# Second block of a two-block transformer layer: the q_b projection tiles go last, preparation of the delta chunks moves beside them, ScalarE takes the key scalings, and TensorE's chunk work is reordered

## What is computed

```python
proj = h @ w_in
(qkv_a, z_a, b_a, a_a, q_b, ckv, z_b, iq, ik, iw) = split(proj)
qkv = silu(causal_conv(qkv_a, conv_w)); q, k, v = split(qkv)
q = l2norm(q) * DK ** -0.5; k = l2norm(k); beta = sigmoid(b_a)
g  = -exp(a_log) * softplus(a_a + dt_bias); gc = cumsum(g)          # in each chunk
decay = exp(where(causal, gc[:, None] - gc[None, :], -inf))
lmat  = where(strict, (k * beta) @ k.T * decay, 0)                  # then (I + lmat)^-1
attn  = (q @ k.T) * decay
qg = q * exp(gc);  kg = k * exp(gc[-1] - gc);  vb = v * beta;  kb_g = k * beta * exp(gc)
```

## Time and profile before

| | |
|---|---|
| median of 3 runs | 2002.6 us (2000.28 to 2003.87) |
| the profiled execution | 1995.06 us, span 1992.9 us, mean granted TensorE clock 0.963 |
| busy in the span | PE 1866.0 us (94%), DVE 1514.0 (76%), ACT 1118.4 (56%), POOL 194.1 (10%) |
| the twelve last split tiles | to about 1762 us of the span |
| biases, g sums, four chunks | about 1762 to 1814 us |
| doubling and the attention of the second mixer | about 1814 to 1930 us |

### The profile page before, as it was taken

One profiled execution on the slowest core, in us unless ns is written; L12 is line 12 of the kernel. 1 busy time (PEld: TensorE's weight loads), 2 busy tenths in 40 slices (PEclk: granted clock), 3 DMA queues, 4 the chain that ended last, 5 costly groups with the idle time before them and its releaser, 6 DMA issues. The chain is left out here.

```text
span 1992.9 us, 24544 instructions
## 1 busy us (share of the span) xinstructions
PE 1866.0 (94%) x8417; PEld 1398.4 (70%) x8418; DVE 1514.0 (76%) x1725; ACT 1118.4 (56%) x1162; POOL 194.1 (10%) x199
## 2 busy tenths in 40 slices
PE   6978978999999999999999999999998999977998
PEld 3346456787777777777787777778774467866983
DVE  4146666999999899899999988998896377866532
ACT  4233315777777777777777767777754344322510
POOL 0031210000000000000000000000143001003410
PEclk9988978999999999999999999999998889988999
DMA  7100836999999999999999999999977212201001
GB/s 211 65 21 11 341 137 226 373 360 369 376 352 368 384 359 373 375 356 374 378 365 377 377 352 371 376 353 383 361 265 239 81 43 70 79 0 64 1 22 42
DMA packets 102007, 499.72 MB, mean 251 GB/s; under 512 B 18611, under 2 KB 35232, under 8 KB 51684
## 3 DMA queue, kind: packets, MB, share of 16 engines
q1 hardware_dynamic: 94898, 473.37, 62.0%
q0 software_dynamic: 7056, 25.69, 3.6%
HBM read 478.57 MB, written 20.46 MB: 250 GB/s over the span
## 5 line engine op out<-in xcount | busy, mean ns | idle before, releaser
L1627 DVE TENSOR_TENSOR part<-ring,part 128x2048 fp32r<-128x2048 f32 x380 | 858.1, 2289 | 108.6 <-ACT part L1348 107.6
L1348 ACT ACTIVATE part<-ring 128x2048 fp32r<-128x2048 f32 x380 | 729.1, 1921 | 331.8 <-DMA ring<-in_w_gate_up 192.2
L1477 PE MATMUL bank<-part,xT_hi 128*128 128x512 f32 x2048 | 535.0, 403 | 20.1 <-DVE xT_lo L1658 15.2
L1477 PEld LDWEIGHTS bank<-part,xT_hi 128*128 128x128 f32 x2048 | 380.9, 190 | 116.0 <-issue 30.6
L1488 PE MATMUL bank<-part,actT_hi 128*128 128x512 f32 x1024 | 280.4, 395 | 0.3 <-ACT rest L1371 0.3
L1477 PE MATMUL bank<-part,xT_lo 128*128 128x512 f32 x1024 | 280.2, 395 | 0.0
L1477 PEld LDWEIGHTS bank<-part,xT_lo 128*128 128x128 f32 x1024 | 193.2, 189 | 45.7
L1488 PEld LDWEIGHTS bank<-part,actT_hi 128*128 128x128 f32 x1024 | 190.2, 188 | 41.7 <-ACT rest L1371 0.5
L1488 PE MATMUL bank<-part,actT_lo 128*128 128x512 f32 x512 | 159.5, 393 | 0.0
L1771 POOL DMA_INDIRECT rest<-h_rows,rest x33 | 43.1, 1305 | 1110.9 <-PE bank L1460 1094.4
L1488 PEld LDWEIGHTS bank<-part,actT_lo 128*128 128x128 f32 x512 | 96.3, 188 | 21.6
(11 more groups left out here) (459 smaller groups left out, 2303.6 us busy)
## 6 DMA issues: line engine op xcount, KB each, us to landing
ring<-in_w_gate_up SPq DMA_DIRECT2D x256, 1024.0 KB, 7.2
ring<-in_w_down SPq DMA_DIRECT2D x128, 1024.0 KB, 6.8
expert_rows<-rest SPq DMA_DIRECT2D x31, 512.0 KB, 7.6
ring<-in_w_in SPq DMA_DIRECT2D x14, 1024.0 KB, 5.2
rest<-in_w_ada SPq DMA_DIRECT2D x8, 1536.0 KB, 6.8
ring<-in_w_out SPq DMA_DIRECT2D x16, 512.0 KB, 4.9
ring<-in_w_in SPq DMA_DIRECT2D x8, 464.0 KB, 7.1
rest<-in_x SPq DMA_DIRECT2D x4, 512.0 KB, 6.4
```

The costliest lines, as they stand in the source:

```text
L1348: nc.scalar.activation(hi[part(i, c)], raw(c), ACT.Copy).then_inc(sig("hi_ready"), counts)
L1477: ins = nc.tensor.matmul(bank[g][:], rows[:, c, :], w[:, g * 512:(g + 1) * 512], start=first, stop=last, skip_group_check=True)
L1627: V.tensor_tensor(lo[part(i, c)], raw(c), hi[part(i, c)].bitcast(F32), ALU.subtract).then_inc(sig("lo_ready"), counts)
```

## The change

- `GROUPS2` puts z_a and z_b ahead of q_b, so the z tiles come first and q_b last.
- TensorE makes the g sums right after `q_rows`, with one more matmul for the chunk totals; turns the biases after the ninth tile; and makes the rows of chunks 0 and 1 after the tenth and the eleventh.
- Rows lie in banks 2 and 3 (even chunks) or 4 and 5 (odd), scores in banks 0 and 1. For each chunk TensorE now issues scores, then turns, then the rows of the chunk two further on. The turns of a chunk wait for `kg_ready` and `beta_v_ready` of the chunk before, the rows for `decay_row_ready` and `LT_ready` of the chunk two back.
- ScalarE multiplies `diff` by `k_scale` (four 128x128 copies a chunk) and makes `wT` and `kg` from the turned keys (eight a chunk). VectorE's `LT` and `AT` are then one 128x512 instruction where they were four of 128x128. The exponents of the totals and of gc are taken once for all chunks.
- `diff` and `decay_row` move off `step_L` and `cross`, and GpSimd's wait for `qg_ready` goes.
- The `choose` rounds are 12 in the first loop, 20 in the z loop, and 16 behind it, between the small steps and `diff_of(0)` and `diff_of(1)`. The four q scalings move from z tiles 0 to 3 to z tiles 4 to 7.

```diff
-GROUPS2 = (3208, 0, 512, 1024, 2056, 1536, 2696)
+GROUPS2 = (3208, 0, 512, 1024, 1536, 2696, 2056)
...
-                    pool.wait_ge(sig("qg_ready"), T)
...  (ScalarE)
+            def exp_diff(t):
+                act.wait_ge(sig("diff_ready"), t + 1)
+                chain.link(A.activation(diff[:, t % 2], diff[:, t % 2], ACT.Exp))
+                act.wait_ge(sig("scales_ready"), 1)
+                for h in range(HA):
+                    ins = A.activation(diff[:, t % 2, h, :], diff[:, t % 2, h, :], ACT.Copy, scale=k_scale[:, t, h:h + 1])
+                ins.then_inc(sig("decay_ready"), 1)
+            def exp_rows(t):
+                if t >= 2:
+                    act.wait_ge(sig("qg_ready"), t - 1)
+                A.activation(decay_row[:, t % 2], heads(2 + 2 * (t % 2)), ACT.Exp).then_inc(sig("decay_row_ready"), 1)
...  (after tile n of the last twelve)
+                if n == 8:
+                    for h in range(HB):
+                        act.wait_ge(sig("bias_done"), h + 1)
+                        A.activation(bias[:, h, :], bank[4 + h % 2][:], ACT.Copy).then_inc(sig("bias_turned"), 1)
+                    act.wait_ge(sig("gc_ready"), 1)
+                    A.activation(eg, gc, ACT.Exp)
+                    A.activation(gl, gl, ACT.Exp)
+                    A.activation(egl, egl, ACT.Exp).then_inc(sig("eg_ready"), 1)
+                if n >= 10:
+                    exp_diff(n - 10)
+                    exp_rows(n - 10)
+            def scale_k(t):
+                act.wait_ge(sig("kv_turned"), t + 1)
+                act.wait_ge(sig("kv_scales"), 1)
+                for h in range(HA):
+                    A.activation(wT[:, t, h, :], heads(6)[:, h, :], ACT.Copy, scale=bg[:, t, h:h + 1])
+                    ins = A.activation(kg[:, t, h, :], heads(6)[:, h, :], ACT.Copy, scale=egl[:, t, h:h + 1])
+                ins.then_inc(sig("kg_ready"), 1)
             for t in range(T):
+                if t + 2 < T:
+                    exp_diff(t + 2)
+                    exp_rows(t + 2)
+                scale_k(t)
...  (TensorE)
+            for n in range(12):
+                split_tile(8 + n // 2, n % 2)
+                if n == 3:
+                    rows_of_q()
+                    sum_g()
+                if n == 8:
+                    turn_bias()
+                if n in (9, 10):
+                    chunk_rows(n - 9)
+            pe.wait_ge(sig("tile_read"), 29)
             for t in range(T):
-                chunk_products(t)
+                chunk_scores(t)
+                turn_kv(t)
+                if t + 2 < T:
+                    chunk_rows(t + 2)
...  (VectorE, behind the z loop)
+            chain.link(V.tensor_copy(gc, bank[6][:, 0:16].rearrange("p (t h) -> p t h", t=T)))
+            V.tensor_copy(gl, total)
+            V.tensor_tensor(egl, total, gc, ALU.subtract).then_inc(sig("gc_ready"), 1)
+            for _ in range(4):
+                choose(next(rounds))
+            dve.wait_ge(sig("eg_ready"), 1)
+            V.tensor_tensor(bg, beta_k, eg, ALU.mult)
+            V.tensor_tensor(egl, egl, k_scale, ALU.mult).then_inc(sig("kv_scales"), 1)
+            for _ in range(6):
+                choose(next(rounds))
+            diff_of(0)
+            for _ in range(4):
+                choose(next(rounds))
+            diff_of(1)
+            for _ in range(2):
+                choose(next(rounds))
             for t in range(T):
...
+                chain.link(V.tensor_tensor(LT[:, t], heads(0), diff[:, t % 2], ALU.mult))
+                V.tensor_tensor(LT[:, t], LT[:, t], heads(b1), ALU.mult).then_inc(sig("LT_ready"), 1)
+                V.tensor_tensor(AT[:, t], heads(1), diff[:, t % 2], ALU.mult).then_inc(sig("chunks_ready"), 1)
                 dve.wait_ge(sig("decay_row_ready"), t + 1)
                 V.tensor_tensor(qgT[:, t], qkvT[:, 0:4, t * P:(t + 1) * P], decay_row[:, t % 2], ALU.mult).then_inc(sig("qg_ready"), 1)
+                scale_v(t)
+                if t + 2 < T:
+                    dve.wait_ge(sig("chunks_ready"), t + 1)
+                    diff_of(t + 2)
```

More of the change, by code:

```diff
@@ L2377, in _ @@
-            for h in range(HB):
-                act.wait_ge(sig("bias_done"), h + 1)
-                A.activation(bias[:, h, :], bank[4 + h % 2][:], ACT.Copy).then_inc(sig("bias_turned"), 1)
-            for t in range(T):
[L2382 to L2390, removed]
+                    A.activation(square[:, n % 2, :], dst, ACT.Sigmoid).then_inc(sig("z_sigm"), 1)
@@ L2548, in _ @@
[L2548 to L2576, removed]
+            def sum_g():
+                pe.wait_ge(sig("g_ready"), 1)
+                pe.wait_ge(sig("ckv_ready"), 1)
+                for t in range(T):
+                    M.matmul(bank[6][:, 4 * t:4 * t + 4], upper, g[:, t, :], start=True, stop=True, skip_group_check=True)
+                M.matmul(bank[6][:, 16:32], ones, g.rearrange("p t h -> p (t h)"), start=True, stop=True, skip_group_check=True).then_inc(sig("gc_done"), 1)
@@ new lines, in rows_of_q, with turn_bias @@
+            def rows_of_q():
+                pe.wait_ge(sig("scales_ready"), 1)
+                pe.wait_ge(sig("relu_ready"), 3 * HI)
+                for t in range(T):
+                    for h in range(HA):
+                        ins = M.matmul(bank[2 + t][:, h * P:(h + 1) * P], q_scale[:, t, h:h + 1].broadcast_to([P, P]), ident, start=True, stop=True, skip_group_check=True)
+                    ins.then_inc(sig("q_rows"), 1)
+            def turn_bias():
+                pe.wait_ge(sig("levels_loaded"), 16)
+                pe.wait_ge(sig("bias_loaded"), 64)
+                pe.wait_ge(sig("ckvT_ready"), 1)
+                pe.wait_ge(sig("q_scaled"), T)
+                for h in range(HB):
+                    if h >= 2:
+                        pe.wait_ge(sig("bias_turned"), h - 1)
+                    M.matmul(bank[4 + h % 2][:], levels[:, 7, :], bias[:, h, :], start=True, stop=True).then_inc(sig("bias_done"), 1)
@@ L2898, in _, with diff_of, scale_v @@
             V.tensor_tensor(beta_k, beta, k_scale, ALU.mult).then_inc(sig("scales_ready"), 1)
[L2899 to L2904 removed]
+            def diff_of(t):
+                dve.wait_ge(sig("rows_done"), t + 1)
+                for h in range(HA):
+                    ins = V.scalar_tensor_tensor(out=diff[:, t % 2, h, :], in0=heads(2 + 2 * (t % 2))[:, h, :], scalar=gc[:, t, h:h + 1], in1=levels[:, 8, :], op0=ALU.subtract, op1=ALU.min)
+                ins.then_inc(sig("diff_ready"), 1)
+            def scale_v(t):
+                dve.wait_ge(sig("kv_turned"), t + 1)
+                V.tensor_tensor(u_sb[:, t], heads(7), spread(beta[:, t, :], P), ALU.mult).then_inc(sig("beta_v_ready"), 1)
             for n in range(8):
                 dst = (z_a, z_b)[n // 4][:, n % 4, :]
[L2907 removed]
+                for _ in range(2 + n % 2):
                     choose(next(rounds))
```

100 lines of the change are left out of this document (35 added, 65 removed).

## The result

The changed kernel takes 1985.84 us in the median (1983.5 to 1987.28, four runs) against 2003.23 us for the kernel before (2000.28 to 2006.62, four runs): ratio 0.991, 95% interval 0.989 to 0.9931. That is 17.4 us less where 10.8 were forecast. Two later comparisons, on two chips, gave 0.9921 (0.9903 to 0.994, 6 runs against 20) and 0.9938 (0.9918 to 0.9959, 10 against 15), or 13.4 and 12.4 us less. One execution of the old kernel (in e1) took 4845.55 us and is left out of all figures. The profiled execution took 1985.49 us, span 1983.7, so 9.2 us less span than the profiled one before.

What follows compares the result with a forecast made beforehand. TensorE bounds the last tiles, VectorE close behind; a handover chain bounds the stage after. Tiles end 9.6 us later, yet the doubling starts at 1803.1 instead of 1813.86: 2002.6 - 10.8 = 1991.8 us, range 1985.5 to 1999.

Steps and rivals of the forecast that it cites:

- The bound and the chain: Between last projection tile and doubling: engines hand over in a 52.1 us chain; the new late place is `kg_ready`.
- The tile stage: Last projection tiles: tile 11 ends at 1771.5, 9.6 us later than before, including a 0.9 us stall ahead of the biases.
- the sum: Added-up chain from tiles through chunks: doubling starts at 1803.1 instead of 1813.86, 10.8 us less.
- ScalarE's prices: New scaled copies in the chunk stage: 0.26 us each from a bank, 0.28 on `diff`; 1.1 us for `diff`, 2.1 for keys.
- TensorE's clock: Chunk stage: a middle between full and half rate, rows 2.8, scores 2.7, turns 1.3 us; clock between 0.6 and 0.9.
- The bounds: Whole kernel: chain ends between -15.3 and -4.1 us; with the spread of runs, a range of 1985.5 to 1999 us.
- cheapest chain: Chunk stage with TensorE at the full clock throughout and 0.25 us a copy: ends at 1798.6, -15.3 us.
- Cheap handovers: Rival, chunk stage: TensorE keeps the full clock through its waits, copies cost 0.25 us; -13 to -15.3 us; chance 0.18.
- VectorE or the key copies bind: Rival, tiles and chunks: copies at 0.35 us, or VectorE's rounds start late; -4 to -8 us; chance 0.16.
- The chain only changes its links: Rival, chunk stage: each of some ten handovers costs 1 us more; within 4 us of 2002.6; chance 0.07.
- It doesn't do what it says: Rival: VectorE reaches `diff_of(1)` 5 us late, chunk 1 isn't prepared beside tiles; gain about 6 us; within the 0.16 case.
- slower: Rival, chunk stage: ScalarE's serial program holds `kg_ready` and the turns; at 0.64 us a copy, 2007 us; chance 0.06.

Runs made afterwards that it cites:

- e1: The kernel before, rerun without an edit beside the kernel before: median 1997.63 us against 1997.79, ratio 0.9996.
- e2: The changed kernel, rerun without an edit, against the kernel before on one chip: 1984.37 us against 1997.79, ratio 0.9921.
- e10: The changed kernel, rerun without an edit, against the kernel before on a third chip: 1986.02 us against 1998.46, ratio 0.9938.
- e4: The changed kernel with six choose rounds put back into the first tile loop: 1989.57 us, ratio 0.9947 to the kernel before.
- e7: The changed kernel with rows, diff and exponents of chunks 0 and 1 moved behind tile 11: ratio 0.9936 to the kernel before.

## Why the prediction was right and where it was wrong

**The bound and the chain: right.** The stage was a chain of handovers, and the new late place is the one named, `kg_ready`, with two waits of 4.0 us where about 4 were forecast.

**The tile stage: right.** Tile 11 was to end 167.1 us after the first split matmul (1771.5 - 1604.4); it ended after 166.9, 168.2 and 166.6. The stall ahead of the biases was 0.9 in the sum and 1.1 in the trace. VectorE was to begin chunk 0's products at 1775.0; it did at 1775.72 (L3000), with a start of the tiles 1.5 us later. From there to the first turn the sum has 28.1 us and this execution 28.55; part of that agreement is luck, since it got the lowest clock of the three (27.3 us in e2, 26.1 in e10).

**ScalarE's prices: right.** 0.25 us a copy from a bank where I took 0.26, 1.19 us for the four on `diff` to the next start (1782.42 - 1781.23) where I took 1.1. The table load showed no drain:

```profile
1753.08 1.28 ACT L2396 ACT_TABLE_LOAD   x1
1754.37 0.21 ACT L2396 ACTIVATE rest<-rest 128x16 f32<-128x16 f32 x1
```

The exponent starts 1.29 us after the load began. The Trainium skill (ScalarE: Activation LUTs, What ACT_TABLE_LOAD costs) has 2.66 us for a switch. By this row it took 1.29, and here the measurement decides.

**TensorE's clock: the term that was mis-sized.** The sum has 12.2 us for TensorE's part of the chain: rows of chunk 2 (2.8), turns of chunk 1 and rows of chunk 3 (4.1), turns of chunk 2 and scores of chunk 3 (4.0), turns of chunk 3 (1.3). These six pieces took 12.3 us in the first profile, 11.2 in e2 and 9.5 in e10, 11.0 in the mean. I called the terms the middle between the rates, and they aren't: between my own 0.11 and 0.19 us a pass the middle is 2.4 us for 16 passes and 1.2 for 8, in all 10.8. Measured, 16 passes took 1.86 us at the full rate (1777.28 to 1779.14) and 3.42 at the half rate (1786.87 to 1790.29). The half rate throughout would have cost 3.3 us over the sum and not 4.0; no run had it.

So the stage is 31.5, 30.3 and 29.1 us long where the sum had 31.6, at clocks of 0.83, 0.89 and 0.94 where I had named 0.6 to 0.9. It is -21.7 us in the mean against my -20.3. With 0.5 us less in the rest, which I had at nothing, and 0.6 us less in the tiles, the sum is -13.2 instead of -10.8 us. The Trainium skill (TensorE: Matmul & The Clock Gate, What's actually happening) holds that activity releases the throttle; the runs agree as far as they go: the order with short waits has 0.99, the one with two waits of 4 us 0.83 to 0.94.

**The bounds: wrong.** The step that failed is the allowance for the measurement. I let the range reach 1.8 us under its cheapest chain, because the three runs of the median lay within 3.6 us. My own table had the warning: the profiled execution was 7.5 us under that median. The old kernel's executions spread over 17 us and its medians in four comparisons over 8. In the profiles the scatter lies ahead of the change and goes with the waits for the expert weights. The median of 1985.84 is a hair above my low end of 1985.5, but 0.991 of the 2002.6 that I built on is 1984.6, under it, and the 17.4 us are more than the cheapest chain gave, 15.3. The later differences, 13.4 and 12.4 us, are inside. Of the 6.6 us by which the first comparison passed the forecast, 2.4 are found in the stages; the other 4.2 are in no profile, and how they divide between scatter and edit stays open. 12 to 13 us is what the profiles and the two later comparisons support.

**The rivals.** *Cheap handovers* asked for TensorE at the full clock. One execution of the change as written came near it (e10: clock 0.94, 15.4 us less from start to end than the old kernel's mean), and with one line moved both profiles had it, for 22 us less. *VectorE or the key copies bind*: VectorE had no slack, but taking its rounds away gained only 0.2 us (e4), since TensorE's scores came at the same time; the copies cost 0.25 us and not 0.35. *The chain only changes its links*: it did change its link, to ScalarE, but the handovers cost no more than I took for them. *It doesn't do what it says*: I had the gain at about 6 us without the early preparation, some 5 less; e7 lost about 1. The mechanism of the *slower* rival was real, ScalarE's serial program holding the turns; only its price was far from the turning point of 0.64 us a copy. I named that place and didn't draw the conclusion: while reading ScalarE's order I should have put its idle 4.9 us beside its eight waiting copies.

## What to carry to other kernels

When work moves to an idle engine, place it in that engine's program where its inputs are ready, ahead of whatever waits for a later input: behind the wait the same eight copies cost TensorE two waits of 4.0 us, and the stage 8 to 10 us with the clock; ahead of it both waits are gone. Work prepared early is worth only the time by which it would have been late, which was 1 us here, since VectorE was busy meanwhile. If a stage ahead waits on DMA, compare stages between profiles from a common event, and give a range the spread of many executions, not of three.

## What was not expected of the hardware

The expert stage, whose code is the same in all fourteen profiles, ended between 1493.3 and 1501.2 us from starts about 3 us apart. TensorE's clock differed between executions of one program over one and the same stage, 0.83 to 0.94. It didn't always fall during a wait: in e10 the turns behind the wait of 4.01 us still ran at 0.11 us a pass, and the rows behind them fell to the half rate.

A VectorE product of two SBUF operands took 0.68 us alone and 1.13 and 1.28 when it began while a GpSimd mask was running, at the start of the doubling (changed kernel). GpSimd's mask took 1.09 us there and 1.40 and 1.47 when it began while such a VectorE product was running, in the chunk stage; the product kept its 0.68. So in these four overlaps only the one that began second took longer.
